# A router computed tile by tile beside the output projection, and nine weight buffers in the second expert layer

## The reference, cut to what matters

```python
x = x + jnp.einsum('bse,ed->bsd', y, w_out[l])
h2 = rms_norm(x, norm2_g[l]).reshape(bsz * seq, d)
...
logits_c = jnp.einsum('nd,dg->ng', h, w_coarse, preferred_element_type=f32)
...
grp = jnp.argmax(logits_c, axis=-1).astype(jnp.int32)
...
logits_f = jnp.einsum('nd,de->ne', h, w_fine, preferred_element_type=f32)
...
top_val, top_idx = lax.top_k(logits_f, TOP_K_FINE)
...
return (jax.nn.silu(xe @ w_gate[e]) * (xe @ w_up[e])) @ w_down[e]
```

## Time and profile before

| | |
|---|---|
| runs | 1944.12, 1948.53, 1949.76 us |
| the profiled execution | 1950.82 us, span 1948.8 us |
| PE busy | 1726.8 us (89%) |
| DVE busy | 624.8 us (32%) |
| ACT busy | 472.5 us (24%) |
| mean over the span | 265 GB/s |
| chain that ended last | PE 74%, DMA 12%, DVE 8%, ACT 3% |

### The profile page before, as it was taken

How to read it: one execution, slowest core, us unless ns; L and a number is a source line. 1 busy time by engine, 2 the same in 40 slices (tenths; PEclk the granted TensorE clock), 3 DMA queues, 4 the chain that set the end, 5 groups by cost and what they waited for, 6 DMA issues and landing times.

```text
span 1948.8 us, 21476 instructions
## 1 busy us (share of the span) xinstructions
PE 1726.8 (89%) x8586; PEld 886.0 (45%) x8586; DVE 624.8 (32%) x1173; ACT 472.5 (24%) x809; POOL 170.1 (9%) x172
## 2 busy tenths in 40 slices
PE   6999999679999999999499989994798999899980
PEld 2455564434445555555255459843333333333330
DVE  3277121232213213112388655523211111111105
ACT  2232551213312112111457213303011111111111
POOL 0000000011111111110000230000111111111110
PEclk9999999779999999999699989996899999999995
DMA  9273711539999999997720631164579999999974
GB/s 345 86 260 130 260 45 43 194 140 400 391 403 412 405 401 404 403 411 290 285 106 0 75 64 44 62 262 173 215 301 407 353 389 371 409 370 375 422 317 162
DMA packets 94042, 515.79 MB, mean 265 GB/s; under 512 B 22381, under 2 KB 28109, under 8 KB 69368
## 3 DMA queue, kind: packets, MB, share of 16 engines
q1 hardware_dynamic: 82744, 497.01, 65.9%
q0 software_dynamic: 11200, 17.39, 2.7%
HBM read 506.64 MB, written 27.05 MB: 274 GB/s over the span
## 4 chain that ended last, share of the span: by engine, by line
PE 74%; DMA 12%; DVE 8%; ACT 3%; SPq 2%; issue 2%; POOLq 0%; DVEq 0%; POOL 0%; ACTq 0%
PE bank L832 22%; PE bank L848 10%; PE bank L472 9%; PE bank L447 8%; DMA ring<-in_w_up 8%; PE bank L780 3%; PE bank L819 3%; PE bank L736 2%; PE bank L440 2%; PE bank L859 2%; PE bank L691 2%; PE bank L530 1%; PE bank L1164 1%; PE bank L1172 1%; DMA ring<-in_w_down 1%
## 5 line engine op out<-in xcount | busy, mean ns | idle before, releaser
L832 PE MATMUL bank<-ring,arena 128*64 128x512 f32 x1104 | 508.3, 615 | 36.2 <-DMA ring<-in_w_up 33.0
L834 PE MATMUL bank<-ring,arena 128*64 128x512 f32 x1104 | 508.6, 615 | 0.0
L832 PEld LDWEIGHTS bank<-ring,arena 128*64 128x64 f32 x1104 | 150.2, 141 | 332.2 <-issue 324.6
L2324 DVE TENSOR_TENSOR arena<-arena,bank 64x512 f32<-64x512 f32 x70 | 48.3, 690 | 693.8 <-ACT arena L1697 693.8
L848 PE MATMUL bank<-ring,arena 128*64 128x512 f32 x552 | 251.6, 598 | 1.6 <-DMA ring<-in_w_down 1.1
L850 PE MATMUL bank<-ring,arena 128*64 128x512 f32 x552 | 251.6, 598 | 0.0
L447 PE MATMUL bank<-arena,ring 128*128 128x512 f32 x560 | 246.4, 596 | 0.0
L1697 ACT ACTIVATE arena<-bank 64x512 f32<-64x512 f32 x70 | 41.2, 589 | 566.1 <-PE bank L834 566.1
L1363 POOL DMA_INDIRECT arena<-xnd,smalli x70 | 67.3, 962 | 1174.6 <-PE bank L819 616.2
L447 PEld LDWEIGHTS bank<-arena,ring 128*128 128x128 f32 x560 | 106.0, 191 | 129.2 <-issue 129.1
L834 PEld LDWEIGHTS bank<-ring,arena 128*64 128x64 f32 x1104 | 150.1, 141 | 0.0
(11 more groups left out here) (428 smaller groups left out, 1816.0 us busy)
## 6 DMA issues: line engine op xcount, KB each, us to landing
ring<-in_w_gate SPq DMA_DIRECT2D x63, 2048.0 KB
ring<-in_w_up SPq DMA_DIRECT2D x63, 2048.0 KB
ring<-in_w_down SPq DMA_DIRECT2D x63, 2048.0 KB
ring<-in_w_mod SPq DMA_DIRECT2D x12, 2048.0 KB
ring<-in_w_in SPq DMA_DIRECT2D x10, 2048.0 KB
ring<-in_w_out SPq DMA_DIRECT2D x4, 2048.0 KB
arena<-yd SPq DMA_DIRECT2D x16, 512.0 KB, 7.1
arena<-in_w_in SPq DMA_DIRECT2D x2, 2048.0 KB, 11.7
```

Source lines behind the costliest of these rows:

```text
L832: pe.matmul(GU[0:CAP, :], x, wg_[:, c, :], start=(c == 0), stop=(c == KD - 1), skip_group_check=True)
L834: mm = pe.matmul(GU[CAP:2 * CAP, :], x, wu_[:, c, :], start=(c == 0), stop=(c == KD - 1), skip_group_check=True)
```

## The change

Two things are changed, and small ones beside them.

First, the router works on one tile of tokens at a time, in the order that `with_tokens` writes out: PE transposes the raw x tile (`turn_tile`) and computes its logits (`logit_tile`) between the products of the projection's right half. The norm's gain is multiplied into the router's weights `rw` beforehand (and in block two the scale; the shift's logits are computed once, as the product `shift`, and added to the bias); 1/rms is applied to the logits by DVE (`logit`). ACT computes it for each tile by Ln and Exp (`tokens`), while DVE scales tiles for `xnd` (`normed`), the last one only after `picked`. The ranks come from five products in place of fourteen, the counts of further blocks from one compare and one reduction, and the slots' product is split: the gather's indices first, the scatter's afterwards.

Second, the second layer has no held expert: its stream cycles through nine buffers, the six of the ring and the three arena parts (`NBUF`, `SPOT`, `ARENA`, `home`), and a load waits for the matrix nine places earlier (`spent`). hT3 moves to another part of the arena.

```diff
-        STREAM = [[], []]
+        STREAM = [[], [(0, 0), (1, 0), (0, 1), (1, 1), (2, 0), (0, 2), (1, 2), (2, 1), (2, 2)]]
...
+        NBUF = 9
+        SPOT = [0, 1, 2, 3, 4, 6, 7, 5, 8]
+        ARENA = [0, 3, 2]
+        def home(m, j, p):
+            i = STREAM[m].index((j, p))
+            rows = 4 if j == 2 else KD
+            if m == 0:
+                return unit(U_MOE[0] + i, rows), landed(U_MOE[0] + i)
+            spot, turn = SPOT[i % NBUF], i // NBUF
+            if spot < RING:
+                sem, count = landed(U_MOE[1] + spot)
+                return unit(U_MOE[1] + spot, rows), (sem, count + 16 * turn)
+            sem, earlier = ((S("ctx_in"), 1), (S("ctx_w"), 2), (S("held"), 0))[spot - RING]
+            return area(ARENA[spot - RING], 0, UNIT).rearrange("p (c n) -> p c n", c=rows), (sem, 16 * (earlier + turn + 1))
...
+        def spent(m, j, p):
+            return S("gu_done") if j < 2 else S("y_done"), BASE[m] + LASTB[m][p] + 1
...
-        hT3 = chunks(area(3, 0, 4096), T)
+        hT3 = chunks(area(4, 0, 4096), T)
...
+            def turn_tile(m, t):
+                pe.wait_ge(V.free, V.at(f"out{'AB'[m]}1{t}"))
+                for half in range(2):
+                    b = C.deal(pe, f"turn{m}{t}{half}")
+                    for j in range(4):
+                        k = 4 * half + j
+                        mm = pe.transpose(hd(b, j), x_tok[:, t, P * k:P * k + P], M["ident"])
+                    mm.then_inc(C.full, 1)
+            def logit_tile(m, t):
+                b = V.deal(pe, f"logits{m}{t}")
+                pe.wait_ge(C.free, C.at(f"turn{m}{t}1"))
+                for k in range(KD):
+                    mm = pe.matmul(b[:, 0:NR], hT3[:, k, P * t:P * t + P], rw[:, m, k, :], start=(k == 0),
+                                   stop=(k == KD - 1))
+                mm.then_inc(V.full, 1)
+            def with_tokens(m, order, part):
+                t0, t1, t2, t3 = order
+                part(t0)
+                part(t1)
+                turn_tile(m, t0)
+                part(t2)
+                turn_tile(m, t1)
+                logit_tile(m, t0)
+                turn_tile(m, t2)
+                part(t3)
+                logit_tile(m, t1)
+                turn_tile(m, t3)
+                logit_tile(m, t2)
+                logit_tile(m, t3)
...
-                        for t in range(TT):
-                            part(t, (4, 5, 6, 7, 0, 1, 2, 3), True)
+                        with_tokens(0, range(TT), lambda t: part(t, (4, 5, 6, 7, 0, 1, 2, 3), True))
...
-                for t in range(TT):
-                    for s in range(t + 1):
-                        pe.matmul(b[:, NE * t:NE * t + NE], M["lt"] if s == t else M["ones"], pick[:, s, :],
-                                  start=(s == 0), stop=(s == t))
+                pe.matmul(b[:, 0:NE * TT], M["lt"], pick_all, start=True, stop=False, skip_group_check=True)
                 for s in range(TT):
-                    mm = pe.matmul(b[:, NE * TT:NE * TT + NE], M["ones"], pick[:, s, :],
-                                   start=(s == 0), stop=(s == TT - 1))
+                    mm = pe.matmul(b[:, NE * (s + 1):NE * TT + NE], M["ones"], pick_all[:, 0:NE * (TT - s)], start=False,
+                                   stop=(s == TT - 1), skip_group_check=True)
...
+                for c in range(2 * TT):
+                    mm = pe.matmul(b[0:CAP, 0:NBLK[m] + 1], in_place[:, c, :], from_block[m][:, c, :],
+                                   start=(c == 0), stop=(c == 2 * TT - 1))
+                mm.then_inc(V.full, 1)
...
+            b = V.deal(pe, "shift")
+            pe.wait_ge(S("gains"), 2)
+            for k in range(KD):
+                mm = pe.matmul(b[:, 0:NR], mBn[:, k:k + 1].to_broadcast([P, P]), rw[:, 1, k, :], start=(k == 0),
+                               stop=(k == KD - 1))
             mm.then_inc(V.full, 1)
...
-                sp.wait_ge(*used_by[k - RING])
+                dst, (sem, _) = home(m, j, p)
+                if m == 0:
+                    sp.wait_ge(*used_by[U_MOE[0] + i - RING])
+                elif i >= NBUF:
+                    sp.wait_ge(*spent(m, *STREAM[m][i - NBUF]))
+                elif SPOT[i] < RING:
+                    sp.wait_ge(*used_by[U_MOE[1] + SPOT[i] - RING])
                 src = w[p] if e is None else w[bass.ds(e, 1)].rearrange("e p c n -> (e p) c n")
-                sp.dma_start(unit(k, src.shape[1]), src).then_inc(S(f"weights{k % RING}"), 16)
+                sp.dma_start(dst, src).then_inc(sem, 16)
...
+                    sp.wait_ge(V.full, V.at(f"outA1{TT - 1}"))
+                    sp.dma_start(hTc, a["ctxT"].rearrange("(c p) t -> p c t", p=P)).then_inc(S("ctx_in"), 16)
+                else:
+                    sp.wait_ge(V.free, V.at(f"outB1{TORDER[-1]}"))
+                    load_e(1, 6)
+                for i, t in enumerate(TORDER if m else range(TT)):
+                    sp.wait_ge(S(f"xn{m}"), i + 1)
                     sp.dma_start(xnd[m][P * t:P * t + P, :], xn_tok[:, t, :]).then_inc(S("xn_out"), 16)
...
+            def tokens(m, order):
+                act.preload_act_table_set(LN_EXP)
+                for t in order:
+                    act.wait_ge(V.free, V.at(f"out{'AB'[m]}1{t}"))
+                    chain(A(xn_tok[:, order[-1], :], x_tok[:, t, :], ACT.Square, accum_out=ssq[:, t:t + 1]))
+                    for half in range(2):
+                        A(hT3[:, 4 * half:4 * half + 4, P * t:P * t + P], chunks(take(f"turn{m}{t}{half}")[:, :], P),
+                          ACT.Copy).then_inc(C.free, 1)
+                    chain(A(rstd[:, t:t + 1], ssq[:, t:t + 1], ACT.Ln, bias=eps, scale=1.0 / D))
+                    A(rstd[:, t:t + 1], rstd[:, t:t + 1], ACT.Exp, scale=-0.5).then_inc(S("rms_ready"), 1)
...
+            TTo(rw[:, 0], rw[:, 0], bc(pcol("g2n", 0, KD), 2, [P, KD, NR]), ALU.mult)
...
+                t = order[i]
+                TS(xn_tok[:, t, :], x_tok[:, t, :], rstd[:, t:t + 1], None, ALU.mult).then_inc(S(f"xn{m}"), 1)
+            def logit(m, order, i):
+                t = order[i]
+                b = take(f"logits{m}{t}")
+                dve.wait_ge(S("rms_ready"), 2 * TT * m + i + 1)
+                if m:
+                    STT(lg[:, t, :], b[:, 0:NR], rstd[:, t:t + 1], pcol("rbias", 0, NR), ALU.mult, ALU.add)\
+                        .then_inc(V.free, 1)
+                else:
+                    TS(lg[:, t, :], b[:, 0:NR], rstd[:, t:t + 1], None, ALU.mult).then_inc(V.free, 1)
...
+                many = key[:, 0:NE] if m else cnt
+                o3 = [P, NE, T // CAP - 1]
+                chain(TTo(over, bc(many, 2, o3), bc(pcol("slot0", 1 - m, T // CAP - 1), 1, o3), ALU.is_gt))
+                chain(dve.tensor_reduce(nov, over, AX, ALU.add))
...
-                chain(TTo(in_, at_[:, :, 0:nblk], at_[:, :, 1:nblk + 1], ALU.subtract))
-                TTo(in_, in_, bc(pcol("tokf", 0, 2 * TT), 2, [P, 2 * TT, nblk]), ALU.mult)
+                chain(TTo(from_, at_, bc(pcol("tokg", 0, 2 * TT), 2, at3), ALU.mult))
```

More of the change, by code:

```diff
@@ L29 @@
 FIXED = 3
-HELD = 2
 TWICE = 6
@@ L221, in build @@
             STREAM[m].append((2, NE - 1))
[L222 to L243, removed]
+            assert sorted(STREAM[m]) == [(j, p) for j in range(3) for p in range(NE)]
+        NBUF = 9
+        SPOT = [0, 1, 2, 3, 4, 6, 7, 5, 8]
@@ L824, in gate_up @@
                     u, p = n % 2, BLOCKS[m][n][0]
-                    wg_, wu_ = (weights(m, j, p) for j in range(2))
+                    wg_, wu_ = (home(m, j, p)[0] for j in range(2))
                     pe.wait_ge(S("xs_ready"), n0 + n + 1)
@@ L1857, in _ @@
             o_turned(3)
[L1859 to L1860 removed]
+            tokens(1, TORDER)
             experts(1)
@@ L2176, in _, with experts @@
                     o = x_tok[:, t, 512 * n:512 * n + 512]
+                    if n and t == TT - 1:
+                        logit(0, range(TT), 0)
                     TTo(o, take(f"outA{n}{t}")[:, :], o, ALU.add).then_inc(V.free, 1)
-            def norm_tok(i, m):
-                dve.wait_ge(S("rms_ready"), i)
-                chain(dve.reciprocal(rstd, rstd))
-                for t in range(TT):
-                    TS(xn_tok[:, t, :], x_tok[:, t, :], rstd[:, t:t + 1], None, ALU.mult).then_inc(S(f"xn{m}"), 1)
-            def experts(m):
-                gain, shift = mAp, (mBp if m else None)
-                thin(f"logits{m}", NR, [T], logitsT)
-                b = take(f"logits{m}")
-                L3 = b[:, 0:TT * NR].rearrange("p (t n) -> p t n", n=NR)
-                if m:
-                    TTo(lg, L3, bc(pcol("rbias", 0, NR), 1, [P, TT, NR]), ALU.add).then_inc(V.free, 1)
-                else:
-                    CP(lg, L3).then_inc(V.free, 1)
-                own(f"logits{m}")
+                    if n and t:
+                        normed(0, range(TT), t - 1)
+            def experts(m, order):
+                gain, shift = mAp, (mBp if m else None)
```

(17 more changed lines are left out.)

217 lines of the change are left out of this document (83 added, 134 removed).

## The result

The changed kernel took 1889.45 us (median of 4 runs, 1876.61 to 1895.6) beside 1947.06 for the kernel before (4 runs): a ratio of 0.9696, 95% interval 0.9643 to 0.9749. It is 57.6 us faster. The forecast was 1869 with a range from 1857 to 1893: the direction and the wide range held. The narrower forecast, 1857 to 1881, to which I had given 0.65, did not: 57.6 us are 27% less than the 79.4 us that I had summed up. The measured time is that of the first rival, 1890, and the range reached it only because the upper values of two rivals had been added.

What follows compares the result with a forecast made beforehand. Bounds: two hand-overs from output projection to first expert block, and the second expert stage, losing about 50 us to weight waits. Savings 8.4 + 14.2 + 10.8 + 48 - 2 = 79.4 from 1948.5 gave 1869 us, range 1857 to 1893.

Steps and rivals of the forecast that it cites:

- the first rival: Second expert stage: loads get only 400 GB/s, 5.4 us each, so the stage gives 27 us; 1890 us, chance 0.20.
- two rivals: Starved load stream (1890 us, chance 0.20) and tile-by-tile routing giving half, 16 us less (1885 us, chance 0.07).
- Logits, layer one: Projection's second half to router logits, layer one: tile-by-tile work takes 40.0 us, logits at 368.2 instead of 376.6, saving 8.4.
- Logits, layer two: Same stretch in layer two: logits at 1328.0 instead of 1342.2, saving 14.2 us.
- the rule on transposes: Router stretch: transposes don't reach full clock, so each layer would give 4 us less; weighed but not adopted.
- Logits to gather: From logits to the first gather, each layer: shorter reductions, ranks, counts and slots save 5.4 us, bounds 4.5 and 6.5.
- Shift product: Added 16 records ahead of block two's first projection: costs 2 us, bounds 0 and 3.6.
- The ring: Second expert stage: nine buffers instead of six let loads run ahead, saving 48 of about 50 us lost.
- the break-even: Second expert stage: load time, 5.15 us each, at which 87 loads just meet the time the last weights are wanted.
- The limit of 358 GB/s: Second expert stage: guide's HBM-to-SBUF bound for a core; 191 MB would take 533 us and the ring gain 0.
- Starving gathers: Second expert stage: indirect gathers starve behind nine queued loads, making the kernel slower than before; chance 0.02.
- My list: Hand schedule of the second expert stage's 87 loads and 38 blocks at 5.0 us a load; no waits with nine buffers.

Runs made afterwards that it cites:

- late_load: Changed kernel with the 2 MB wvc load issued only when the first two gathers of layer one have landed; 1884.87 us, ratio 0.9673.
- ring_only: Kernel before the change, with only the nine buffers going round in the second expert stage added; 1922.94 us, ratio 0.9898.
- tiles_only: Changed kernel whose second expert stage keeps the three arena places fixed and cycles six buffers, as before; 1905.95 us, ratio 0.9819.
- vacant_all: Changed kernel with 36 of 38 gathers and all 38 scatters of the second expert layer pointed out of range; 1863.09 us, ratio 0.9581.
- full_gather: Changed kernel with vacant slots of the second layer's gathers fetching the last token's row; 1919.47 us, ratio 0.9871.
- no_gather: Changed kernel with 36 of 38 gathers of the second expert layer pointed out of range, scatters as they are; 1864.40 us, ratio 0.9584.
- no_scatter: Changed kernel with all 38 scatters of the second expert layer pointed out of range, gathers as they are; 1876.55 us, ratio 0.9651.

## Why the prediction was right, and where not

- **Logits, layer one: 8.4 us forecast, 10.2 measured.** From the right half's start to the routing 38.2 us (329.6 to 367.8) in place of 40.0. Eight transposes took 1.04 to 1.07 as booked. A logit tile of 16 records took 1.87 where I had 2.1; the bounds were 7 and 14 for four, and they took 7.4.
- **Logits, layer two: 14.2 forecast, 16.0 measured**, by the same 38.2 us. The clock stayed at 1.00, 2.4 GHz, through both stretches. By the rule on transposes that I had weighed (the Trainium skill, "TensorE: Matmul & The Clock Gate", Part 4) the end might have run at half clock; with transposes set between matmuls the trace doesn't agree.
- **Logits to gather: 5.4 forecast, 5.3 and 5.4 measured** (367.82 to 385.35 against 22.9 us before; 1313.03 to 1335.82 against 28.2 before). The first gather is issued at 385.35; 385.7 was forecast, and that they agree to 0.4 us is partly luck: the projection began 1.3 us later than before, and the logits came 1.8 us sooner than booked. It is released by the slots (DVE L2328), not by the writes to xnd, so their cover, thin as it was, held.
- **After the gather's issue: nothing forecast, 3.9 us lost in layer one.** This is a step that I left out. I followed the DMAs that stand ahead of the gather only as far as the xnd writes. The wvc load waits for those writes. Before, it was issued at 375.58 and had landed long before the gather at 399.50. Now the last write follows `picked`, so the load goes out 7.2 us later, at 382.82, and the gather comes 14.2 us sooner: it ran into the load. `late_load` showed it.
- **Shift product: 2 us booked, 1.97 measured** (16 records at 958.42). The whole stretch around it is 2.0 us shorter all the same. Between the traces of the changed kernel it differs by more than that (201.1 to 204.1), so whether the 2 us reach the end is open.
- **The ring: 48 forecast, 28.6 measured.** The mechanism was right: single places freed late by double blocks, lead as the cure, the break-even near 5.15 us a load. `ring_only` gave 26.2 us of stage, and `tiles_only` lost 25.3. **The term that failed is the price of a load, 5.0 us, read from the tail at 426 GB/s.** In the stage a load took 5.4. From the first free place (1351.5, and the 7 us for restart) to the w_up of the last expert (1817.4) there are 85 loads in 458.9 us, 5.40 each. The rival at 5.4 had said 27 us, though by a slip: its 191 MB at 400 GB/s over 87 loads make 5.49 us each, and by the break-even of 5.15 some 18 us of gain. It named the right term and met 28.6 partly by luck, since the stage moved 410 GB/s from 1370 to 1800 us and not 400. I had looked at how full the engines were in that tail and not at what shared them; the earlier trace rows shows blocks near the end at 15 us each, and their gathers were nearly empty. The remark against the rival, that in layer one PE's pace set the demand, was a wrong defence: a share of 1.00 said that the engines were full there too. The limit of 358 GB/s (the Trainium skill, "DMA: Bandwidth & Descriptors", "Where 436 GB/s comes from") would have given the ring nothing. That section gets it by halving the 716 GB/s of a stack between two cores, and here one core runs: the stage moves 402 to 421, so the trace doesn't agree for this case, and it was right to go by rows. It was wrong to go by the best of them.
- **Starving gathers** did not come: in the stage they land in 8.5 us in the median, against 8.4 in the same stage before (the 9.2 of the earlier trace rows is from layer one's). What I had asked was what the loads do to the gathers; what the gathers do to the loads was the larger effect.
- My list with the rates of the groups gives a stage of 464 to 469 us with nine places, and 474.9 were measured. Against the 455.5 us that the forecast implied (503.5 less 48) the rate explains 9 to 14 of the missing 19.4 us, and `vacant_all` shows that without the transfers all of it comes back. The last 6 to 11 stay open. The list had been short by a like amount on the kernel before, 1873 against 1880.5 for the last start, and the forecast took no account of that gap.

## What to carry to other kernels

Price a stream of loads from a stretch whose other traffic is like that of the stage to be forecast; the fastest stretch of a trace is often fast because something is missing in it. Check the list or model on the kernel at hand first, and carry what it misses there into the range. Where both engines and DMA are nearly full, work out how much a group needs and how much it gets, since a deeper ring only postpones that deficit, and one place may bring most of what three bring. When a step comes sooner, look through every queue for what used to run after it and now runs beside it.

## What the runs showed of the hardware

- Gathers of 4 KB rows cost the loads beside them more than their bytes: 5.55 MB more (`full_gather`, the same row again and again) took 35.2 us, 6.3 us a MB; 3.9 MB less (`no_gather`) gave 21.9 us, at least 5.6 us a MB; 4.2 MB of scatters less (`no_scatter`) gave 8.6 us, 2.0 us a MB, in packets of the same mean size. Beside gathers the loads' packets ran at 391 to 404 GB/s of their own engine time, without them at 418 to 422.
- With a 2 MB load issued 2.5 us ahead of it, the first gather of 64 rows let PE wait 7.2 to 7.8 us in the three traces of the changed kernel; without the load 3.9.
- Gathers and scatters whose rows are all out of range still make their packets (800 in 61 us, `vacant_all`) and take 0.7% of the engines' time.
- Transposes set between matmuls kept the clock at 1.00: 32 transposes in the 38.2 us of either hand-over.
